# Moving the opening work of a two-group encoder kernel between engines, and rewriting its inverse roots

## What is computed

```
def rmsnorm(x, g):
    return x * lax.rsqrt(jnp.mean(x * x, axis=-1, keepdims=True) + EPS) * g

def gla_mixer(h, S0, w_in, w_gate_up, b_gate, head_gain, w_out):
    q, k, v, r, gdown = jnp.split(h @ w_in, [...], axis=-1)
    g = jax.nn.log_sigmoid(gdown @ w_gate_up + b_gate) / GLA_TAU
    S, o = gla_sequence(S0, q, k, v, g)
    o = o * lax.rsqrt(jnp.mean(o * o, axis=-1, keepdims=True) + EPS) * head_gain
    return (o * jax.nn.silu(r)) @ w_out, S

def trunk(x, ...):
    for i in range(2):
        h = rmsnorm(x, norm_mix[i])
        x = x + (gla_mixer(h, ...) if i == 0 else shortconv_mixer(h, ...))
        x = x + conv_ffn(rmsnorm(x, norm_ffn[i]), ...)
    return rmsnorm(x, norm_final)
```

## Time and profile before

| | |
|---|---|
| median of 3 runs | 1559.14 us (1558.96 to 1562.8) |
| time of the profiled execution | 1559.23 us |
| its span, first to last instruction | 1557.4 us |
| mean granted clock of TensorE | 0.995 |
| PE busy | 1527.5 us (98%), 10264 matmuls |
| DVE, POOL, ACT busy | 953.6, 584.9 and 455.4 us |
| DMA | 123.75 MB, mean 79 GB/s |

### The profile page before, as it was taken

One profiled execution on the slowest core, in us unless ns is written; L12 is line 12 of the kernel. 1 busy time (PEld: TensorE's weight loads), 2 busy tenths in 40 slices (PEclk: granted clock), 3 DMA queues, 4 the chain that ended last, 5 costly groups with the idle time before them and its releaser, 6 DMA issues.

```text
span 1557.4 us, 26163 instructions
## 1 busy us (share of the span) xinstructions
PE 1527.5 (98%) x10264; PEld 1506.3 (97%) x10264; DVE 953.6 (61%) x1294; ACT 455.4 (29%) x714; POOL 584.9 (38%) x425
## 2 busy tenths in 40 slices
PE   6999999999999999999999999999999999999996
PEld 5999998799999999999999999999999999999996
DVE  7556665854965556566557544458965556566556
ACT  5345555543211121221225111115222121221222
POOL 5433331144344333433435434336343333433432
PEclk9999999999999999999999999999999999999998
DMA  6211115222222222222222222222222222122212
GB/s 214 74 62 55 55 55 211 116 73 70 66 82 68 80 68 81 67 67 81 69 81 72 86 71 73 83 64 81 68 72 78 70 78 81 63 71 81 68 42 78
DMA packets 34824, 123.75 MB, mean 79 GB/s; under 512 B 3872, under 2 KB 6816, under 8 KB 33600
## 3 DMA queue, kind: packets, MB, share of 16 engines
q1 hardware_dynamic: 31824, 108.37, 21.5%
q10 hardware_dynamic: 2928, 14.35, 2.4%
HBM read 114.48 MB, written 8.22 MB: 79 GB/s over the span
## 4 chain that ended last, share of the span: by engine, by line
issue 49%; POOL 27%; PE 18%; DVE 2%; ACT 1%; DVEq 1%; DMA 1%; POOLq 0%; SPq 0%; ACTq 0%
POOL wl L351 26%; PE ps L429 11%; PE ps L512 2%; PE ps L724 1%; PE ps L564 1%; PE ps L622 1%; POOL sq L380 1%; PE ps L526 1%; DVEq L788 0%; DMA x<-x_t 0%; POOL ol L367 0%; DVE x L1182 0%; DMA s<-states 0%; PE ps L493 0%; PE ps L483 0%
## 5 line engine op out<-in xcount | busy, mean ns | idle before, releaser
L351 POOL TENSOR_TENSOR wl<-raw,wh 128x512 fp32r<-128x512 f32 x390 | 545.0, 1421 | 876.4 <-ACT wh L1265 876.4
L429 PE MATMUL ps<-xh,wh 128*128 128x328 f32 (+5 forms) x2176 | 504.7, 313 | 12.5 <-DVE xl L774 12.5
L429 PE MATMUL ps<-xl,wh 128*128 128x328 f32 (+5 forms) x2176 | 502.4, 312 | 0.0
L429 PE MATMUL ps<-xh,wl 128*128 128x328 f32 (+5 forms) x2176 | 502.2, 312 | 0.0
L429 PEld LDWEIGHTS ps<-xh,wh 128*128 128x128 f32 x2176 | 388.3, 190 | 14.8 <-issue 8.7
L429 PEld LDWEIGHTS ps<-xl,wh 128*128 128x128 f32 x2176 | 389.1, 189 | 0.0
L429 PEld LDWEIGHTS ps<-xh,wl 128*128 128x128 f32 x2176 | 388.9, 189 | 0.0
L1265 ACT ACTIVATE wh<-raw 128x1024 fp32r<-128x1024 f32 x196 | 204.3, 1055 | 319.6 <-PE ps L429 296.8
L823 DVE TENSOR_TENSOR x<-ps,x 128x644 f32<-128x644 f32 (+2 forms) x200 | 158.5, 821 | 69.6 <-PE ps L445 42.6
L1055 DVE TENSOR_TENSOR zp<-ps,rstd 128x520 f32<-128x520 f32 (+1 forms) x88 | 61.1, 694 | 221.1 <-PE ps L429 220.9
L1036 DVE SCALAR_TENSOR_TENSOR y<-zp,par,y 128x660 f32<-128x660 f32 (+1 forms) x192 | 178.8, 932 | 26.5 <-issue 21.7
(11 more groups left out here) (166 smaller groups left out, 1178.6 us busy)
## 6 DMA issues: line engine op xcount, KB each, us to landing
raw<-w_units SPq DMA_DIRECT2D x196, 512.0 KB, 3.5
s<-states ACTq DMA_DIRECT2D x4, 1024.0 KB, 5.8
state_sample<-snew ACTq DMA_DIRECT2D x4, 1024.0 KB, 4.8
x<-x_t SPq DMA_DIRECT2D x8, 328.0 KB, 6.2
x<-x_t ACTq DMA_DIRECT2D x1, 2624.0 KB, 13.6
y_t<-x SPq DMA_DIRECT2D x2, 400.0 KB, 2.5
ffn_last<-zl ACTq DMA_DIRECT2D x2, 396.0 KB, 3.1
y_t<-x SPq DMA_DIRECT2D x2, 360.0 KB, 2.5
```

What stands on the lines that cost most here:

```text
L351: ins = pool.tensor_tensor(wl[:, j, half, :], raw[:, j, half, :], wh[:, j, half, :].bitcast(F32), ALU.subtract)
L429: mm = pe.matmul(ps[:, p, c:c + z - a], w[:, ring, k, :], v[:, k, a:z], start=(k == 0 and w is wh and v is hi), stop=(k == KT - 1 and w is ...
```

## The change

- **Squares and unit 1.** All eight squares of the opening are made by ACT, after all eight `xh` and after `wh` of unit 1. POOL makes none; it begins with `wl` of unit 2.
- **First low parts.** `wh` and `wl` of units 0 and 1 are made in halves of four tiles; both halves of `wl` on DVE. Unit 0's second half comes after the first tile's `xl`; unit 1's two halves come after all `xl` and ahead of the additions of squares. PE starts unit 0 or 1 when its first half is there and waits for the second ahead of the fifth tile.
- **Loads.** Unit 0 is loaded in two halves issued by ACT. SP begins with `par` and the tiles of `x`; unit 1 comes after all of `x`.
- **Norm sum.** `norm_sum(0)` is ahead of the eighth tile of unit 1.
- **Idle products.** PE does 14 products of `ones` by `ones`, 128 x 128, in a slot that is not in use, as soon as `ones` is set.
- **Roots.** All ten: ACT does Ln, Exp, Square of r into `v`, and a Copy of r with scale -0.5/d; DVE does two operations, v = (sum + d EPS) v and r = (v - 3 d) r, where it had four. The table set that holds both Ln and Exp is loaded explicitly, ahead of each norm's root and once ahead of the stage of the heads, just before `ident_of` and the loads of the states.

```diff
@@ sync
-        sp.dma_start(raw[:, 0, :, :], w_in[0]).then_inc(landed[0], 16)
         sp.dma_start(par[:, 0:C_FFN], par_in[:, 0:C_FFN]).then_inc(sem["par_in"], 16)
         for k in range(KT):
             sp.dma_start(x[:, k, :], x_in[:, k, :]).then_inc(x_in_s[k], 16)
-            if k == KT - 3:
-                sp.dma_start(raw[:, 1, :, :], w_in[1]).then_inc(landed[1], 16)
-        sp.dma_start(par[:, C_FFN:], par_in[:, C_FFN:]).then_inc(sem["more_par_in"], 16)
-        for j in (2, 3):
+        for j in range(1, RING):
             sp.dma_start(raw[:, j, :, :], w_in[j]).then_inc(landed[j], 16)
+            if j == 1:
+                sp.dma_start(par[:, C_FFN:], par_in[:, C_FFN:]).then_inc(sem["more_par_in"], 16)
@@ gpsimd
-        pool.memset(ones[:, :], 1.0)
+        pool.memset(ones[:, :], 1.0).then_inc(sem["ones_set"], 1)
...
-        for n, m in enumerate(POOL_SQ):
-            pool.wait_ge(x_in_s[m], 16)
-            pool.tensor_tensor(sq0[:, m, :], x[:, m, :], x[:, m, :], ALU.mult).then_inc(sem["pool_sq_done"], 1)
-        pool.wait_ge(sem["lo_done"], 1)
-        for j in range(1, RING):
+        pool.wait_ge(sem["lo_done"], 2)
+        for j in range(2, RING):
             low(j, j + 1)
@@ tensor
-            return lambda k: norm_sum(n) if k == KT // 2 else None
+            return lambda k: norm_sum(n) if k == (KT // 2 if n else KT - 1) else None
+        pe.wait_ge(sem["ones_set"], 1)
+        for _ in range(WARM_UP):
+            pe.matmul(ps[:, RING - 1, 0:P], ones[:, :], ones[:, :], start=True, stop=True)
@@ vector
+        def inverse_root(step, r, v, d, c=None):
+            n_root = ROOT_ORDER.index(step)
             p = take(step)
-            dve.wait_ge(sem["log_done"], n_root + 1)
             out, src = (two(v), slot(p)) if c is None else (v, bank(p, c))
-            dve.tensor_scalar(out, src, -0.5 / d, par[:, C_HALF_EPS:C_HALF_EPS + 1], ALU.mult,
-                              ALU.add).then_inc(freed[p], 1)
-        def refine(n_root, r, v):
-            dve.wait_ge(sem["root_done"], n_root + 1)
+            dve.wait_ge(sem["root_squared"], n_root + 1)
+            dve.scalar_tensor_tensor(out=out, in0=src, scalar=d * EPS, in1=out, op0=ALU.add,
+                                     op1=ALU.mult).then_inc(freed[p], 1)
             dve.drain()
-            dve.tensor_tensor(v, v, r, ALU.mult)
-            dve.drain()
-            dve.tensor_tensor(v, v, r, ALU.mult)
-            dve.drain()
-            dve.scalar_tensor_tensor(out=r, in0=v, scalar=1.5, in1=r, op0=ALU.add, op1=ALU.mult)
+            dve.wait_ge(sem["root_scaled"], n_root + 1)
+            dve.scalar_tensor_tensor(out=r, in0=v, scalar=-3.0 * d, in1=r, op0=ALU.add, op1=ALU.mult)
             dve.drain()
...
+        first_low(0, 0, "first_hi", "first_lo")
         dve.wait_ge(sem["par_in"], 16)
-        for m in range(KT):
+        split_low(0, 0)
+        first_low(0, 1, "hi_done", "lo_done")
+        for m in range(1, KT):
             split_low(0, m)
-            if 2 <= m < KT - 2:
-                add_square(0, m - 2)
-        for m in range(KT - 4, KT):
+        first_low(1, 0, "first_hi", "first_lo")
+        first_low(1, 1, "hi_done", "lo_done")
+        for m in range(1, KT):
             add_square(0, m)
@@ scalar
-            act.activation(tiny[:, :], ones[:, 0:1], ACT.Ln)
             p = take(step)
             out, src = (two(r), slot(p)) if c is None else (r, bank(p, c))
-            act.activation(out, src, ACT.Ln, scale=1.0 / d,
-                           bias=par[:, C_EPS:C_EPS + 1]).then_inc(sem["log_done"], 1)
+            act.activation(out, src, ACT.Ln, scale=1.0 / d, bias=par[:, C_EPS:C_EPS + 1])
             act.drain()
-            act.activation(r, r, ACT.Exp, scale=-0.5).then_inc(sem["root_done"], 1)
+            act.activation(r, r, ACT.Exp, scale=-0.5)
+            act.drain()
+            act.activation(v, r, ACT.Square).then_inc(sem["root_squared"], 1)
+            act.activation(r, r, ACT.Copy, scale=-0.5 / d).then_inc(sem["root_scaled"], 1)
...
+        act.dma_start(raw[:, 0, 0:KT // 2, :], w_in[0, :, 0:KT // 2, :]).then_inc(sem["first_half_in"], 16)
+        act.dma_start(raw[:, 0, KT // 2:KT, :], w_in[0, :, KT // 2:KT, :]).then_inc(landed[0], 16)
+        act.wait_ge(sem["first_half_in"], 16)
+        first_high(0, 0, "first_hi")
         act.wait_ge(sem["par_in"], 16)
         for m in range(KT):
             act.wait_ge(x_in_s[m], 16)
             split_high(0, m)
-            if m == KT - 2:
-                high(1)
-            if m and m - 1 not in POOL_SQ:
-                square(0, m - 1)
+            if m == 0:
+                act.wait_ge(landed[0], 16)
+                first_high(0, 1, "hi_done")
+                act.wait_ge(sem["consts"], 1)
+                act.dma_start(wgd_raw[:, :, :], wgd_in).then_inc(sem["gla_in"], 16)
+                act.dma_start(wgu[0:32, :], wgu_in).then_inc(sem["gla_in"], 16)
+        act.wait_ge(landed[1], 16)
+        first_high(1, 0, "first_hi")
+        first_high(1, 1, "hi_done")
         act.dma_start(reset[:, :], reset_in).then_inc(sem["gla_in"], 16)
-        square(0, KT - 1)
+        for m in range(KT):
+            square(0, m)
         high(2)
         high(3)
...
         take(("r", HEADS - 1, 1))
+        log_and_exp()
         for parity in range(2):
             ins = act.activation(ident_of[:, parity, :], ident[:, :], ACT.Copy,
```

More of the change, by code:

```diff
@@ L80 @@
 C_FOURTH = 76
-C_EPS, C_HALF_EPS = 80, 81
+C_EPS = 80
 C_PARITY = 82
@@ L418, in weights, with project @@
             pe.wait_ge(sem["lo_done"], n_ready)
-        def project(step, hi, lo, n_ready, ring, first=0, cut=HALF, i=0, release=1, before=None):
+        def project(step, hi, lo, n_ready, ring, first=0, cut=HALF, i=0, release=1, before=None, in_halves=False):
             p = open_slot(step, i)
-            weights(n_ready)
+            if in_halves:
+                pe.wait_ge(sem["first_lo"], n_ready)
+            else:
+                weights(n_ready)
             for k in range(KT):
+                if in_halves and k == KT // 2:
+                    weights(n_ready)
                 if before:
@@ L781, in add_square @@
                 return
-            if n:
-                dve.wait_ge(sem["sq_done"], KT * n - len(POOL_SQ) + m + 1)
-            else:
-                dve.wait_ge(sem["pool_sq_done"], sum(t <= m for t in POOL_SQ))
-                dve.wait_ge(sem["sq_done"], sum(t <= m and t not in POOL_SQ for t in range(KT)))
+            dve.wait_ge(sem["sq_done"], KT * n + m + 1)
             if m > 1:
@@ L1170, in add_first_square @@
             return dve.tensor_tensor(sq[:, 0, half(0)], sq[:, 0, half(0)], sq[:, m, half(0)], ALU.add)
-        def last_half_square(c):
-            dve.wait_ge(sem["log_done"], len(ROOT_ORDER) - 1 + c)
-            dve.tensor_scalar(cg[:, half(c)], ps[:, c, 0:OUT_PARTS[c + 1] - OUT_PARTS[c]], -0.5 / D,
-                              par[:, C_HALF_EPS:C_HALF_EPS + 1], ALU.mult, ALU.add)
         def last_root(c):
-            refine(len(ROOT_ORDER) - 2 + c, rstd[:, half(c)], cg[:, half(c)])
+            n_root = len(ROOT_ORDER) - 2 + c
+            dve.wait_ge(sem["root_squared"], n_root + 1)
+            dve.scalar_tensor_tensor(out=cg[:, half(c)], in0=ps[:, c, 0:OUT_PARTS[c + 1] - OUT_PARTS[c]],
+                                     scalar=D * EPS, in1=cg[:, half(c)], op0=ALU.add, op1=ALU.mult)
+            dve.drain()
+            dve.wait_ge(sem["root_scaled"], n_root + 1)
+            dve.scalar_tensor_tensor(out=rstd[:, half(c)], in0=cg[:, half(c)], scalar=-3.0 * D, in1=rstd[:, half(c)],
+                                     op0=ALU.add, op1=ALU.mult)
             dve.drain().then_inc(sem["final_std"], 1)
@@ L1190, in _ @@
         ins.then_inc(sem["last_sum"], 1)
-        for m in range(3):
+        for m in range(OPEN):
             add_last(1, m)
-        last_half_square(0)
-        add_last(1, 3)
         last_root(0)
@@ L1265, in high, with first_high @@
             act.activation(wh[:, j, :, :], raw[:, j, :, :], ACT.Copy).then_inc(sem["hi_done"], 1)
-        high(0)
-        act.wait_ge(sem["consts"], 1)
-        act.dma_start(wgd_raw[:, :, :], wgd_in).then_inc(sem["gla_in"], 16)
-        act.dma_start(wgu[0:32, :], wgu_in).then_inc(sem["gla_in"], 16)
+        def first_high(j, part, done):
+            rows = slice(part * KT // 2, (part + 1) * KT // 2)
+            act.activation(wh[:, j, rows, :], raw[:, j, rows, :], ACT.Copy).then_inc(sem[done], 1)
+        act.dma_start(raw[:, 0, 0:KT // 2, :], w_in[0, :, 0:KT // 2, :]).then_inc(sem["first_half_in"], 16)
+        act.dma_start(raw[:, 0, KT // 2:KT, :], w_in[0, :, KT // 2:KT, :]).then_inc(landed[0], 16)
+        act.wait_ge(sem["first_half_in"], 16)
+        first_high(0, 0, "first_hi")
         act.wait_ge(sem["par_in"], 16)
@@ L1528, in last_root @@
             act.activation(rstd[:, half(c)], bank(c, 0)[:, 0:OUT_PARTS[c + 1] - OUT_PARTS[c]], ACT.Ln, scale=1.0 / D,
```

(9 more changed lines are left out.)

41 lines of the change are left out of this document (20 added, 21 removed).

## The result

The changed kernel takes 1550.1 us, the median of 5 runs (1549.74 to 1550.87). The kernel before takes 1559.14 beside it (1557.68 to 1562.8). The ratio is 0.9939, with an interval of 0.9927 to 0.9951: faster, and by more than 0.3%. The forecast was 1547.0 with a range of 1543.5 to 1551. So 9.0 us came of the 12.2 in the sum. The profiled execution took 1550.13, its span is 1548.3.

What follows compares the result with a forecast made beforehand. The prediction took PE's number of matmuls to bound 91% of the span. Gains of 7.3 in the opening, 3.3 in the heads and 1.6 at the end, 12.2 us, led from 1559.2 to 1547.0, range 1543.5 to 1551.

Steps and rivals of the forecast that it cites:

- Opening, 7.3: Up to unit 2 on PE: sum of squares done at 24.1, unit 2 at 30.8 instead of 38.13, 7.3 us gained.
- Idle products, 0: PE before unit 0: full rate from the first matmul, but valued at nothing, covered by the wait for the sum of squares.
- Unit 0 on ACT's queue, 0: Loads in the opening: issuing unit 0 from ACT saves only issue time, so nothing in the sum.
- Unit 1 behind x, 1.3: Loads in the opening: last tile of x lands 1.3 us sooner, at 12.9, and unit 1 at 14.2.
- States late, 1.0: Before the heads: the new table load ahead of `ident_of` delays the states' issue, costing 1.0 us.
- The rival by the page, 2.7: Before the heads: the table load with its drain makes the states 2.7 us late; total 1548.7, chance 0.14.
- Heads, 4.3 gross: Stage of the heads: gains of 1.5 chain wait, 0.7 new states, 1.7 clock and 0.4 `ol`; net 3.3 us.
- The end, 1.6: Last norm to last products: shorter root, 2.9 us from the last Ln instead of 3.94; 1.6 us gained in all.
- Middle, 0: Between the heads and the end: PE is busy throughout, nothing in the change alters it, so no gain or loss.
- The rival nothing disturbed (1545.1): Opening and heads: all additions of squares run free of POOL and the states are not late; 1545.1, chance 0.08.
- The other rivals: Opening's gain lost later (1554.3, 0.07); table loads stay between Ln and Exp (1549.8, 0.03); unit 1 landing late, slower (0.02).

Runs made afterwards that it cites:

- e1: The changed kernel's new opening with the old inverse roots everywhere, against the kernel before: 1552.87 us, ratio 0.9954.
- e3: The changed kernel without the 14 idle products: 1549.36 us, ratio 0.9936 to the kernel before.
- e4: The changed kernel with the norm sum ahead of unit 1's fifth tile again: 1554.61 us, ratio 0.9977 to the kernel before.
- e7: The changed kernel with unit 0's two halves issued by SP ahead of `par`, not by ACT: 1551.49 us, ratio 0.9953 to the kernel before.
- e8: The changed kernel with unit 1 loaded between the sixth and seventh tile of x: 1551.16 us, ratio 0.9949 to the kernel before.
- e6: The changed kernel with the addition `osum` on POOL ahead of its `ol`, not on DVE: 1548.77 us, ratio 0.9935 to the kernel before.
- e9: The changed kernel with an unused 64-byte-per-partition tensor where the removed 32-byte one stood: 1548.22 us, ratio 0.9928 to the kernel before.
- e5: The changed kernel with an unused 32-byte-per-partition tensor where the removed one stood: 1548.42 us, ratio 0.993 to the kernel before.
- e11: The changed kernel with POOL waiting for DVE's casts of `wgd` before unit 2's low parts: 1549.04 us, ratio 0.9935 to the kernel before.

## Why the prediction was right, and where its sum was wrong

**Opening, 7.3: right, by its own steps, with luck in one of them (below).** The sum of squares came at 23.4 for 24.1: the squares began 0.7 earlier than I had them, and one addition was disturbed, by 0.9, in place of two by 0.4 each. The rest took the difference back: the norm sum and the last tile 2.3 us for 1.9, and the casts of `wgd`, to which I gave no place, 0.25. The slot of unit 0 was hidden, as forecast: `take_k` started at 29.25; e1 shows what it costs when it isn't.

**Idle products, 0: right** (e3). **Norm sum ahead of the eighth tile:** e4 shows that it is worth 3.6; the prediction gave it no term of its own.

**Unit 0 on ACT's queue, 0: wrong**, 1.84 (e7). The prediction let the page's "only issue time" stand for nothing, but unit 1 is issued 1.44 later without the move, and the squares wait for unit 1. **Unit 1 behind x, 1.3: too much**, 0.76 (e8). The sum of the opening came out since I built it from landings, with 14.2 for unit 1 where 13.63 was measured. With unit 0 on SP the new order alone would have had unit 1 at 15.4, so my 14.2 was 1.2 too early for the order and left out 1.8 for the queue. That the two nearly cancel is luck.

**States late, 1.0: wrong.** The issue didn't move against ACT's Exp (239.08 with Exp at 239.06, before 246.41 with 246.40). The queue issues ahead of the engine by more instructions than I allowed, and the load fell behind it. The rival by the page, 2.7, fell with it.

**Heads, 4.3 gross: too much.** The chain's 1.5 and the clock's 1.7 went as forecast, so 3.2. The 0.7 for the new states did not, and the wait for `ol` grew by 0.4 where I had it vanish: 4.3 - 0.7 - 0.4 - 0.4 = 2.8, of which 2.3 was seen. The wait for the store, 0.7 in this execution and 0.4 in the one before, can be 0.3 of the rest; 0.2 stays open. The step that failed is that the wait for the new states would go with the shorter root: e6 shows that `osum` on DVE holds it, and that addition took as long before the change (2.19, now 2.06). Why `ol` came later was not tested. Net 2.3 for 3.3. The clock's part depends on the execution too: e1 and e9 had half clock in the heads where the changed kernel had none.

**The end, 1.6: 1.3.** The path from Ln was shorter than my 2.9 at 2.58; the products beside POOL gave 0.55 back.

**Middle, 0: wrong**, -1.9. I had looked for waits and for added work in this stretch and rightly found none. What failed is the sentence that nothing in the change alters it: the change moved the addresses of all buffers allocated behind `ones`, and e5 and e9 show that this is the price. With the heads, 1.0 short, this makes most of the 3.1 us by which the gain of the span missed the sum; the time still lies in the range, 0.9 below its upper end, though the range allowed nothing for the middle.

The rival nothing disturbed (1545.1) did not occur as it stood: the sum of squares came nearly as early as it had it (23.4 for 23.2) and the states were not late, but one addition, `osum` and the last products were all disturbed, and the middle took 1.9. The other rivals did not occur: PE shows no new wait between unit 2 and the heads, no table load stands between Ln and Exp, and unit 1 landed at 13.6.

## What to carry to other kernels

When an engine's work is moved, ask which other engine it will run beside: here the same addition cost 0.84 or 0.83 us alone and 1.75 or 2.06 beside GpSimd. Taking the work out of such a meeting gained 1.1 us (e11) and 1.3 (e6) in the medians. Put a wait directly ahead of the instruction that needs it, above all a wait on a store, whose landing varies. And when a change removes or adds a small tensor, measure it once with a pad in its place, so that a shift of addresses isn't booked to the change. And read the granted clock and the waits on stores before comparing two single profiles: each moved the heads by more than 1 us between profiled executions.
